# Layer 2: a and w products in pairs, running sums kept in DRAM, the first batch's lab products and inverse beside conv_out

## The reference

```python
h = rms_norm_2(x, pre_mix_norm[i])
proj = h @ w_in[i]
p_r, p_k, p_v, p_c, z_rwkv, z_conv = jnp.split(proj, splits, axis=-1)
...
w_log = -jax.nn.softplus(-(w0 + jnp.tanh(xw @ w1) @ w2)) - 0.5
decay = jnp.exp(-jnp.exp(w_log))
a = jax.nn.sigmoid(a0 + (xa @ a1) @ a2)
...
def step(S, inp):                       # wkv7, a scan over the 512 tokens
    r_t, w_t, k_t, v_t, a_t, b_t = inp
    sa = jnp.einsum('bhvk,bhk->bhv', S, a_t)
    S = S * w_t[:, :, None, :] + sa[..., None] * b_t[:, :, None, :] + v_t[..., None] * k_t[:, :, None, :]
    y = jnp.einsum('bhvk,bhk->bhv', S, r_t)
    return S, y
...
c = jax.nn.silu(layer_norm(depthwise_conv(u * sigmoid(gate)), ln_w, ln_b))
merged = sigmoid(z_rwkv) * (y_rwkv @ w_o) + sigmoid(z_conv) * (c @ w_conv_out)
x = x + rms_norm_2(merged @ w_out[i], post_mix_norm[i])
```

## Time and profile before

| | us |
|---|---|
| median of 3 runs | 2329.79 |
| the profiled execution, own time | 2331.41 |
| its span | 2329.6 |
| PE busy | 2237.2 (96%) |
| DVE / ACT / POOL busy | 1019.2 / 881.3 / 1023.4 |

### The profile page before, as it was taken

The page is one execution under the profiler, slowest core; times in us unless marked ns, Lnnn a source line. Parts: engine busy times, 40 slices in busy tenths (PEclk is TensorE's granted clock), DMA queues, the critical chain, the costliest instruction groups (busy, mean ns, idle before and its releaser), DMA issues.

```text
span 2329.6 us, 36136 instructions
## 1 busy us (share of the span) xinstructions
PE 2237.2 (96%) x14692; PEld 1843.3 (79%) x14692; DVE 1019.2 (44%) x1655; ACT 881.3 (38%) x1503; POOL 1023.4 (44%) x605
## 2 busy tenths in 40 slices
PE   7999999999999999999998999999968999999998
PEld 6867888888987688888886888877757778888888
DVE  6264622211346644222116698746674455322212
ACT  5264523322423654233224223272535445322322
POOL 4422544444543155444536444444430465444443
PEclk9999999999999999999998999998989999999999
DMA  6601333333252023333333333433201422333332
GB/s 176 149 27 37 86 115 97 100 101 99 74 132 73 2 64 99 93 99 97 100 93 109 101 94 100 143 111 109 82 3 40 146 85 79 109 98 92 94 100 70
DMA packets 386583, 214.08 MB, mean 92 GB/s; under 512 B 36959, under 2 KB 378695, under 8 KB 385907
## 3 DMA queue, kind: packets, MB, share of 16 engines
q1 hardware_dynamic: 383299, 200.88, 30.2%
q0 software_dynamic: 2448, 9.70, 1.1%
q10 hardware_dynamic: 672, 1.18, 0.1%
HBM read 198.75 MB, written 14.51 MB: 92 GB/s over the span
## 4 chain that ended last, share of the span: by engine, by line
PE 86%; DVE 4%; POOL 3%; issue 3%; ACT 3%; DMA 0%; ACTq 0%; POOLq 0%; DVEq 0%
PE ps L2400 25%; PE ps L2401 24%; PE ps L2402 24%; PE ps L2610 2%; PE ps L2585 2%; PE ps L2595 2%; POOL w_lo L848 2%; POOL x_res L915 1%; PE ps L2573 1%; PE ps L2762 0%; ACT w_hi L1039 0%; PE ps L2473 0%; PE ps L2985 0%; PE ps L2907 0%; PE ps L2867 0%
## 5 line engine op out<-in xcount | busy, mean ns | idle before, releaser
L848 POOL TENSOR_TENSOR w_lo<-raw,w_hi 128x1024 fp32r<-128x1024 f32 (+2 forms) x344 | 822.8, 2396 | 887.8 <-ACT w_hi L1039 882.8
L2400 PE MATMUL ps<-h_hi,w_hi 128*128 128x512 f32 (+1 forms) x2048 | 791.1, 386 | 17.0 <-DVE h_lo L1737 4.6
L2402 PE MATMUL ps<-h_lo,w_hi 128*128 128x512 f32 (+1 forms) x2048 | 779.6, 381 | 0.0
L2401 PE MATMUL ps<-h_hi,w_lo 128*128 128x512 f32 (+1 forms) x2048 | 779.5, 381 | 0.0
L1039 ACT ACTIVATE w_hi<-raw 128x1024 fp32r<-128x1024 f32 (+1 forms) x344 | 358.1, 1042 | 1098.4 <-PE ps L2402 1087.4
L2400 PEld LDWEIGHTS ps<-h_hi,w_hi 128*128 128x128 f32 x2048 | 386.4, 189 | 105.4 <-issue 26.5
L2402 PEld LDWEIGHTS ps<-h_lo,w_hi 128*128 128x128 f32 x2048 | 386.6, 189 | 73.4
L2401 PEld LDWEIGHTS ps<-h_hi,w_lo 128*128 128x128 f32 x2048 | 386.9, 189 | 72.1 <-issue 1.6
L2400 PE MATMUL ps<-hid_hi,w_hi 128*128 128x512 f32 (+1 forms) x616 | 222.0, 360 | 0.0
L2402 PE MATMUL ps<-hid_lo,w_hi 128*128 128x512 f32 (+1 forms) x616 | 221.2, 359 | 0.0
L2401 PE MATMUL ps<-hid_hi,w_lo 128*128 128x512 f32 (+1 forms) x616 | 221.2, 359 | 0.0
(11 more groups left out here) (366 smaller groups left out, 2586.1 us busy)
## 6 DMA issues: line engine op xcount, KB each, us to landing
raw<-in_w_gu SPq DMA_DIRECT2D x88, 512.0 KB, 3.8
raw<-in_w_in SPq DMA_DIRECT2D x56, 512.0 KB, 3.9
raw<-in_w_down SPq DMA_DIRECT2D x32, 448.0 KB, 3.5
raw<-in_ffn_w_gate SPq DMA_DIRECT2D x22, 512.0 KB, 3.8
raw<-in_ffn_w_up SPq DMA_DIRECT2D x22, 512.0 KB, 3.8
raw<-in_w_in_b SPq DMA_DIRECT2D x20, 512.0 KB, 3.9
raw<-in_w_down SPq DMA_DIRECT2D x16, 512.0 KB, 3.7
raw<-in_w_out SPq DMA_DIRECT2D x16, 512.0 KB, 3.7
```

The lines of the kernel that those rows point to most:

```text
L848: nc.gpsimd.tensor_tensor(lo[:, k0:, :], src[:, k0:, :], hi[:, k0:, :].bitcast(f32), ALU.subtract).then_inc(lo_done, 1)
L2400: nc.tensor.matmul(bank, wh[:, k, :], ah[:, part], start=first, stop=False)
L2401: nc.tensor.matmul(bank, wl[:, k, :], ah[:, part], start=False, stop=False)
L2402: return nc.tensor.matmul(bank, wh[:, k, :], al[:, part], start=False, stop=end)
```

## The change

a and w products are made together: for each c, `pre_a_and_w` issues a and w for tokens 0 to 255 and then for 256 to 511, a on rows 64 to 127 of the PE array into bank 7, w on rows 0 to 63 into bank 4 (the sums of the layer norm move from bank 4 to 5). ScalarE's `w_of` follows each `a_of` and writes into `cum_stage`, four slots beside the other temporaries; VectorE makes the running sum there (`cum_of`), GpSimd stores two c at a time to a new DRAM scratch in slots 3 to 6, and SP loads all into `u_cum` after z's last panel, ahead of u_v and of conv_out's fifth panel. `EXP_SLOTS` move to slots 15 to 18. Lab products 0 and 1 run after conv_out's panel 4 (`LAB_SLOT`) in banks 4 to 7, and VectorE goes through the inverse of batch 0 before it waits for the stored z. From conv_out's fifth panel to rwkv_out's second the weights use `raw` slots 2 and 3 alone. VectorE's cols and step_of get a copy for each batch, and ScalarE waits for the stored z at the rows product and no longer at the list's start.

```diff
+CUM_STAGES = 4
+CUM_SLOTS = (3, 4, 5, 6)
...
+                            ("cols0", [P, BS, 2, RH], x_off + 12288), ("cols1", [P, BS, 2, RH], x_off + 22528),
...
-        step_of = at("step_of", [P, 2 * C], x_off + 22528)
+        step_of = [at("step_of0", [P, 2 * C], x_off + 12288), at("step_of1", [P, 2 * C], x_off + 22528)]
...
+        cum_stage = at("cum_stage", [P, CUM_STAGES, TOK], x_off + 2112 * 4)
...
+        def raw_slots(p):
+
+            if wide(p):
+                return (1, 2, 3)
+            return (2, 3) if LABS_FROM <= p < L["rwkv_out"].p0 + 2 else (1, 2, 3, 0)
+
+        LABS_FROM = L["conv_out"].p0 + 4
...
+        EARLY = 2
+
         def slot_of(m):
 
-            return (m - len(products)) % 4
+            return m + 2 if m < EARLY else (m - len(products)) % 4
...
-        W_SLOTS = {15: (0, 1, 2), 16: (3, 4, 5), 17: (6, 7)}
-        EXP_SLOTS = {17: (0, 1), 18: (2, 3), 19: (4, 5), 20: (6, 7)}
+        EXP_SLOTS = {15: (0, 1), 16: (2, 3), 17: (4, 5), 18: (6, 7)}
+        LAB_SLOT = 4
...
-                if p == L["conv_out"].p0 + 5:
+                if p == L["conv_out"].p0 + 4:
                     sp.wait_ge(used, L["z"].p1)
+                    for i in range(2):
+                        sp.wait_ge(sg[f"cum_out{i}"], 16 * KD // CUM_STAGES)
+                    for c in range(0, KD, 2):
+                        sp.dma_start(u_cum[:, c:c + 2, :], scratch["cum"][:, c:c + 2, :]).then_inc(sg[f"merge_in{c // 2}"], 16)
...
+                if i in CUM_SLOTS:
+                    c = 2 * CUM_SLOTS.index(i)
+                    pool.wait_ge(sg["cum_ready"], c + 2)
+                    pool.dma_start(scratch["cum"][:, c:c + 2, :], cum_stage[:, c % CUM_STAGES:c % CUM_STAGES + 2, :]
+                                   ).then_inc(sg[f"cum_out{c // 2 % 2}"], 16)
...
             def w_of(c):
                 act.wait_ge(sg["pre_w"], c + 1)
-                act.wait_ge(used, L["z"].p1)
-                nc.scalar.activation(u_cum[:, c, :], ps[:, 4 + c % 3, :], ACT.Sigmoid,
+                if c >= CUM_STAGES:
+                    act.wait_ge(sg[f"cum_out{c // 2 % 2}"], 16 * (c // CUM_STAGES))
+                nc.scalar.activation(cum_stage[:, c % CUM_STAGES, :], ps[:, 4, :], ACT.Sigmoid,
                                      bias=vec("decay_w0_2", c)).then_inc(sg["w_sig"], 1)
 
             def decay_of(c):
-                act.wait_ge(sg["w_sig"], KD)
+                act.wait_ge(sg["kk_ready"], KD)
                 act.wait_ge(sg["rk_kept"], 1)
-                act.wait_ge(sg["cum_ready"], c + 1)
+                act.wait_ge(sg[f"merge_in{c // 2}"], 16)
...
                     a_of(2 * (i - 2))
+                    w_of(2 * (i - 2))
...
-                if i == max(W_SLOTS):
+                if i == min(EXP_SLOTS):
...
+                if kind == "rows":
+                    for par in range(2):
+                        act.wait_ge(sg[f"z_out{par}"], 16 * 3 * KD // 2)
...
+            def cum_of(c):
+                if c == 0:
+                    dve.wait_ge(sg["starts_loaded"], 16)
+                dve.wait_ge(sg["w_sig"], c + 1)
+                w = cum_stage[:, c % CUM_STAGES, :]
+                nc.vector.tensor_tensor_scan(w, starts[:, :], w, 0.0, ALU.mult, ALU.add).then_inc(sg["cum_ready"], 1)
...
+            for c in range(3):
+                cum_of(c)
             add_up(u_w, lambda c: dve.wait_ge(sg["conv_sq"], c + 1))
+            cum_of(3)
+            cum_of(4)
             rstd()
+            cum_of(5)
...
+            cum_of(6)
+            cum_of(7)
...
-            dve.wait_ge(sg["starts_loaded"], 16)
-            for c in range(KD):
-                dve.wait_ge(sg["w_sig"], c + 1)
-                nc.vector.tensor_tensor_scan(u_cum[:, c, :], starts[:, :], u_cum[:, c, :], 0.0, ALU.mult, ALU.add
-                                             ).then_inc(sg["cum_ready"], 1)
-            for c in range(KD):
-                scale_by_decay(dve, c)
-
-
-            dve.wait_ge(sg["x_out"], 16)
-            dve.wait_ge(sg["b_tilde"], KD)
-
-            for par in range(2):
-                dve.wait_ge(sg[f"z_out{par}"], 16 * 3 * KD // 2)
-            nc.vector.memset(state[:, :, :], 0.0).then_inc(sg["state_clear"], 1)
-            dve.wait_ge(sg["w_sig"], KD)
-            for row in (rows_hi, rows_lo):
-                nc.vector.tensor_scalar(row[:, :], u_r[:, 0, :], 0.0, None, ALU.mult).then_inc(sg["head_rows_clear"], 1)
...
+            dve.wait_ge(sg["b_tilde"], KD)
+            dve.wait_ge(lo_done, max(p for p in range(L["rwkv_out"].p0 + 2) if raw_slot[p] in (0, 1)) + 1)
+            for m in range(EARLY):
+                for part in range(2):
+                    lab_out(m, part)
+            for q in range(NB):
+                gather(0, q)
+            turn_blocks(0)
+            link(block_inverse(nc.vector, link, 0))
+            blocks_back(0)
+            dve.wait_ge(sg["blocks_back"], 1)
+            dve.wait_ge(used, L["conv_out"].p1)
+            spread_blocks(nc.vector, 0).then_inc(sg["tri_first"], 1)
+
+            for par in range(2):
+                dve.wait_ge(sg[f"z_out{par}"], 16 * 3 * KD // 2)
+            nc.vector.memset(state[:, :, :], 0.0).then_inc(sg["state_clear"], 1)
             dve.wait_ge(sg["state_clear"], 1)
+            nc.vector.tensor_scalar(rows_hi[:, :], state[:, :, :].rearrange("p c n -> p (c n)"), 0.0, None, ALU.mult
+                                    ).then_inc(sg["head_rows_clear"], 1)
...
-            def pre_a(c):
+                chunk_sums(u_w[:, 0, :], True, True, bank=5)
+
+            def pre_a_and_w(c):
                 if c == 0:
                     pe.wait_ge(sg["w2a2_loaded"], 16 * 2)
                     pe.wait_ge(sg["lora_ready"], 2)
                 else:
                     pe.wait_ge(sg["a_ready"], c)
-                nc.tensor.matmul(ps[:, 7, :], wa2[64:128, c * P:(c + 1) * P], lora_wa[64:128, :], start=True, stop=True
-                                 ).then_inc(sg["pre_a"], 1)
-
-            def pre_w(c):
-                if c == 0:
-                    pe.wait_ge(sg["kk_ready"], KD)
-                if c >= 3:
-                    pe.wait_ge(sg["w_sig"], c - 2)
-                nc.tensor.matmul(ps[:, 4 + c % 3, :], wa2[0:64, c * P:(c + 1) * P], lora_wa[0:64, :], start=True, stop=True
-                                 ).then_inc(sg["pre_w"], 1)
+                    pe.wait_ge(sg["w_sig"], c)
+                for half in range(2):
+                    part = cols_of(half)
+                    a = nc.tensor.matmul(ps[:, 7, part], wa2[64:128, c * P:(c + 1) * P], lora_wa[64:128, part], start=True, stop=True)
+                    w = nc.tensor.matmul(ps[:, 4, part], wa2[0:64, c * P:(c + 1) * P], lora_wa[0:64, part], start=True, stop=True)
+                a.then_inc(sg["pre_a"], 1)
+                w.then_inc(sg["pre_w"], 1)
...
+            def early_labs():
+
+                pe.wait_ge(sg["b_tilde"], KD)
+                pe.wait_ge(sg["k_tilde"], KD)
+                for m in range(EARLY):
+                    lab_product(products[m][1], (2 * slot_of(m), 2 * slot_of(m) + 1))
+
+            project("conv_out", between={LAB_SLOT: early_labs})
```

More of the change, by code:

```diff
@@ L589, in block_inverse @@
                 shape = [P, n, 2, k]
-                step = step_of[:, 0:2 * n * k].rearrange("p (i q j) -> p i q j", q=2, j=k)
+                step = step_of[batch][:, 0:2 * n * k].rearrange("p (i q j) -> p i q j", q=2, j=k)
                 below = rows[:, k + 1:, :, 0:k]
@@ L2119, in _ @@
                                       ).then_inc(sg["pick_ready"], 1)
+            for c in range(KD):
+                scale_by_decay(dve, c)
             def heads(bank):
@@ L2152, in turn_blocks @@
             def turn_blocks(batch):
-                nc.vector.transpose(wk["rows"][:, :, :, :], wk["cols"][:, :, :, :]).then_inc(sg["blocks_turned"], 1)
+                nc.vector.transpose(wk["rows"][:, :, :, :], wk[f"cols{batch}"][:, :, :, :]).then_inc(sg["blocks_turned"], 1)
                 dve.wait_ge(sg["blocks_turned"], batch + 1)
@@ L2185, in _ @@
                     if kind == "lab":
-                        written(dve, product, part)
-                        dst = wk["lab"][:, i, :, :].rearrange("p (g e b) n -> p e b g n", e=2, b=2)[:, part]
-                        nc.vector.tensor_tensor(dst, ps[:, bank, :].rearrange("p (b g n) -> p b g n", b=2, n=C),
-                                                mask(M_STRICT, [P, 2, 4, C]), ALU.mult).then_inc(bank_out[bank], 1)
-                        if i % 2 and part:
-                            batch = i // 2
-                            if batch == 0:
-                                for q in range(NB):
-                                    gather(batch, q)
-                                turn_blocks(batch)
-                                link(block_inverse(nc.vector, link))
-                                blocks_back(batch)
-                                dve.wait_ge(sg["blocks_back"], 1)
```

(11 more changed lines are left out.)

69 lines of the change are left out of this document (40 added, 29 removed).

## The result

| | before | after |
|---|---|---|
| median of the runs, us | 2328.27 (2325.64 to 2331.19, 4 runs) | 2309.3 (2309.15 to 2309.58, 4 runs) |
| ratio, 95% interval | | 0.9918 [0.9901, 0.9936] |
| profiled execution: own time, span | 2331.4, 2329.6 | 2309.15, 2307.4 |
| first z_stage | 1497.6 | 1495.9 |
| rk_sums' second block starts | 1618.8 | 1619.0 |

The kernel is 19.0 us faster by the medians, 22.2 by the two spans. The forecast was 2305, range 2297 to 2316. The profiled execution of before lay 3.1 us above the median of all its runs; that is the difference between 22.2 and 19.0.

The account below looks back on a forecast made before the run. TensorE was taken to bound the kernel (86% of the span), with a 17.0 us wait for `wk_tri`. 2331.4 - 25.9 + 0.8 = 2306.3, less 1.6 for the profiled execution's excess, gave 2305, range 2297 to 2316.

Parts of the forecast that it names:

- Part 1, w products: Around conv_out's start: 10.0 us of w products leave PE; beside a in z's panels they cost 0.8.
- The rival without overlap: z panels: PE's row halves don't overlap, so w products cost 7.6 instead of 0.8; 2312, chance 0.10.
- The cover: z's panels: added sigmoids, scans and stores fit beside PE's work, cost 0; otherwise some 1 us at each of four places.
- Part 2, conv_out: conv_out starts behind rk_sums at 1619.8, labs after panel 4 cost 1.9 without waiting, end 1668.4, 8.0 us sooner.
- the clock stayed at 1.00: After z: clock kept and VectorE hindered less, conv_out left at 1665.7, 31 us gained; 2298 to 2299, chance 0.14.
- the 2.7 that I charged: conv_out's first panel: the clock falls once more, costing 2.7 us, so panel 4 ends at 1650.0 instead of 1647.3.
- Part 3, the inverse: First batch's inverse on VectorE beside conv_out: 15.5 us after the masks unhindered, plus 9.4 of GpSimd blocking; z masked from 1681.8.
- `wk_tri` comes at 1678.4: End of the first inverse's spread on VectorE: 1669.0 unhindered, plus 9.4 us for four w_lo and the unit diagonal.
- caught more often than once per w_lo: VectorE's inverse: small operations caught more often, or w_lo held up so PE waits; another 9.4 us, 2314, chance 0.13.
- The sum: Whole kernel: 2331.4 - 25.9 + 0.8 = 2306.3; the profiled execution lay 1.6 above the median, so 2304.7, 2305.
- Starved weights: conv_out's panels wait for loads with two raw slots; at 20 us per load 37 lost, 2342; chance 0.03.
- Only the w products go: First batch: wk_tri is early but something equally late is waited for; only 10 us gained, 2320, chance 0.05.

Follow-up runs that it names:

- e3: Changed kernel with each w product as one 512-column matmul two chunks behind its a product; 2317.67 us.
- e10: The changed kernel measured a second time, with nothing edited; 2310.68 us, ratio 0.9934 to the kernel before.
- e5: Changed kernel with the four unit diagonals of column groups 0 and 1 shrunk to one column of one head, output wrong; 2304.38 us.
- e2: Changed kernel with the first two lab products and the inverse moved back behind conv_out's panel 7; 2316.47 us.
- e9: Changed kernel with w products apart from a products and the first lab products and inverse behind conv_out; 2325.95 us, ratio 0.9995 to the kernel before.
- e1: Changed kernel with GpSimd adding the unit diagonals only after VectorE has spread the first inverse (wk_tri); 2306.95 us.
- e8: Changed kernel with the unit diagonals made once the inverted rows are back (blocks_back), ahead of wk_tri's spread; 2305.19 us.
- e11: Changed kernel with the unit diagonals waiting for blocks_back, timed once more beside the changed kernel; 2306.41 us.

## Why the prediction was right, and where its terms were off

**Part 1, w products.** Right, and charged too high: 0.8 us for eight pairs, where the distance of the a product's slots says 0.36 for seven of them, with a wait of 0.3 in it (the first slot is 1.71 us earlier than before, the last 1.35). The rival without overlap is excluded by e3: apart they cost 8.4. The cover held: from 1500 to 1545 PE waits 0.3 us once, for a sigmoid of w on ScalarE; GpSimd waits 3.2 us for the running sums, and the one w_lo that came late, at 1547, was 0.2 late, as one was before (0.24, at 1554).

That 256 columns in two halves are neither dearer nor cheaper than 512 answers the rule weighed there, of the Trainium skill, TensorEngine Tiling (Array Packing), section Instruction Overhead: by its 60 cycles 16 more matmuls would cost an estimated 0.4 us. The trace shows 1.06 against 1.05 us for a pair, 0.01, so the rule isn't seen here.

**Part 2, conv_out.** The structure was right: start behind rk_sums, labs without a wait, 2.0 us (1647.42 to 1649.44). conv_out ended at 1666.1 rather than 1668.4, because the clock stayed at 1.00, 2.4 GHz, from 1620 to 1630. I had put that at 0.14, as a rival, since the thin stretch ahead of it is unchanged. In this profile it was luck: in the second one of the same kernel (e10) the clock fell behind rk_sums, as in eight of the ten variants, but for 3.5 us instead of 10, and cost 1.6 us instead of the 2.7 that I charged. So the term was mis-sized, and neither 2.7 nor 0 is its usual value. What the argument lacked: one trace shows one place and one length of the fall. In the traces of before, after and the eleven experiments it falls once to three times between 1583 and 1634, at places that differ even between kernels with the same instructions up to there (after: 1583 to 1591 and 1597 to 1601; e10, the same kernel: 1596 to 1603 and 1620 to 1624), and the mean from 1576 to 1640 is 0.87 to 0.97. 0.05 of 64 us at full speed is 3.2 us. The runs scatter with the clock: of e10's six the one at 2304.71 us had a mean granted clock of 0.989, the one at 2317.18 of 0.981; how much of that arises in this stretch isn't shown. Here the changed kernel lost at 1583 to 1602 what it kept at 1620; its rk_sums came no earlier than before, though z had started 1.7 us earlier.

**Part 3, the inverse.** The step that failed in size is "`wk_tri` comes at 1678.4". Unhindered the 28 small operations are 7.8 us; three catches were to add 7.2 and the spread 1.2. They took 20.4 (1658.00 to 1678.36). The catch on the gathers cost 0.9 (forecast 1.0), the next two 2.0 and 2.5 (2.4 each), but the last cost 8.1 instead of 2.4, and the spread was not caught. What the forecast had wrong is where GpSimd's unit diagonals strike: it let them meet the spread, for 1.2, and they kept out a small operation that had begun beside the w_lo ahead of them. With conv_out 2.3 us earlier, `wk_tri` was still 2.3 later than forecast, so the term is 4.6 too small, and e5, in which z starts 5.6 sooner, gives its size from the other side. I had written the rule as "waits for the end of the GpSimd instruction"; here the operation waited through six GpSimd instructions in a row. That isn't a general rule either, since before and in e2 VectorE got in between the same four diagonals; what decides it stays open. The small rival, "caught more often than once per w_lo", didn't come true: the catches were as many as forecast, one of them three times the length. The Trainium skill's rule in SBUF - State Buffer, section Who interferes with whom, says that the loser waits for the other's whole instruction: the short catches agree (0.9, 2.0 and 2.5 us beside w_lo blocks of 2.4, and 1.2 us each beside the diagonals of before), the long one (8.37 us, through six instructions) goes beyond it.

The memset, rows_hi and the masks of lab 2, 3 behind the spread were the next limit as forecast: from 1680.7 to 1684.0, 3.3 us, forecast 3.4.

**The sum.** Forecast for the gain up to the mask of z: 25.9, less 0.8 for the pairs, 25.1; measured 23.6 (1707.6 to 1684.0). With the 0.8 conv_out was to end at 1669.2 and `wk_tri` to stand at 1679.2. conv_out ended 3.1 sooner, 2.7 of it by the kept clock, and the inverse took back 4.6. Two errors of opposite sign, then, and the first is luck: with e10's fall of the clock the miss would have been an estimated 1.6 us larger, though still inside the range. Behind the mask the gain was to stay; at the reciprocal it is 22.5, at the span's end 22.2, so 1.4 were lost. The clock fits the 1.1 lost up to the reciprocal, for its mean over these 119 us is 0.96 where it was 0.97 and 0.01 of them is 1.2 us, but no run isolates it (windows, after and before):

```profile
1684.00:1802.80 118.80, 103.71 (x3313) 94.56 (x3307) 58.59 (x87) 58.69 (x108) 22.92 (x37) 0.96 0.13 39
```

```profile
1707.70:1825.30 117.60, 102.18 (x3329) 93.29 (x3323) 58.23 (x86) 58.91 (x109) 22.70 (x37) 0.97 0.13 40
```

The profiled execution of after took 2309.15 where 2306.3 was forecast for it. I then took 1.6 off, since that of before lay so far above its median; that of after lay at its median, and the 1.6 are the rest of the miss. In terms of the parts as e9 shows them: not paying for the w products 8.4, early inverse 7.2, everything else 1.0 or nothing.

**Rivals.** Starved weights: PE waits for w_hi or w_lo nowhere from 1600 to 1700; the window of conv_out's first panel moved 388 GB/s and cost nothing. "Only the w products go" (2320) is what e2 comes near to, 2316.5: without the early slot the time would have been there.

## What to carry to other kernels

A thin matmul that uses 64 rows is free beside another on the other 64 rows (1.06 us for the pair against 1.05 for one), if it is issued as its direct neighbour; two chunks apart it cost its full 1.05. So look for such pairs before looking for a place in a gap. A chain of short VectorE operations in SBUF should not only be counted against GpSimd's long instructions one by one: one of them can be kept out through several in a row (8.37 us here), though it need not be (1.2 us behind each diagonal in e2). No run with a pause of GpSimd behind the w_lo had the long catch (e1, e8, e11), but moving GpSimd's later work behind the chain pays only until that work is itself what is waited for. A clock that falls in one trace gives no fixed term; take a second trace, or the mean over a stretch, before charging it.
